# A hybrid decoder trunk on one core: a reworked router chain with the second expert's later loads held behind the first gather, and the last norm with ScalarE taking the moments of five tiles

## The reference

```
scores = softmax(x @ router_w + router_b)                      # 1024 tokens x 16 experts
grouped = scores.reshape(n_tok, 4, 4)
group_score = sum(top_k(grouped, 2)[0], -1)
sel = argmax(group_score)                                      # one group for each token
top_vals, top_idx = top_k(grouped[sel], 2)                     # two experts of that group
gates = top_vals / sum(top_vals)
moe = sum over the two experts of gate * ((silu(x @ w_gate[e]) * (x @ w_up[e])) @ w_down[e])
out = layer_norm(alpha * x + moe, ln2_g, ln2_b)                # mean and variance over 1024 columns
```

## Time and profile before

| | |
|---|---|
| runs | 1371.47, 1374.96, 1375.51 us |
| profiled execution | 1372.77 us, span 1370.7 us |
| granted clock, mean | 0.971 |
| PE busy | 1268.2 us (93%) |
| DVE busy | 511.4 us (37%) |
| ACT busy | 349.3 us (25%) |
| POOL busy | 108.1 us (8%) |
| moved by DMA | 170.17 MB, mean 124 GB/s |

### The profile page before, as it was taken

One profiled execution on the slowest core, in us unless ns is written; L12 is line 12 of the kernel. 1 busy time (PEld: TensorE's weight loads), 2 busy tenths in 40 slices (PEclk: granted clock), 3 DMA queues, 4 the chain that ended last, 5 costly groups with the idle time before them and its releaser, 6 DMA issues.

```text
span 1370.7 us, 23143 instructions
## 1 busy us (share of the span) xinstructions
PE 1268.2 (93%) x9642; PEld 628.1 (46%) x9642; DVE 511.4 (37%) x934; ACT 349.3 (25%) x482; POOL 108.1 (8%) x177
## 2 busy tenths in 40 slices
PE   7999999999999999999999964999999999999960
PEld 3444444444577777777445532333333333333320
DVE  3035310344178887886355355111111111110118
ACT  1044302234134433345221112111111111111114
POOL 1000000000111111010000001011101010101010
PEclk9999999999999999999999986999999999999985
DMA  5110010010000000001704008866789499397135
...
DMA packets 61012, 170.17 MB, mean 124 GB/s; under 512 B 3184, under 2 KB 3312, under 8 KB 60928
## 3 DMA queue, kind: packets, MB, share of 16 engines
...
...
## 4 chain that ended last, share of the span: by engine, by line
PE 86%; DVE 5%; ACT 4%; DMA 2%; issue 2%; SPq 0%; POOL 0%; POOLq 0%; DVEq 0%; ACTq 0%
PE PS L1762 32%; PE PS L204 19%; PE PS L1251 8%; PE PS L643 6%; PE PS L213 3%; PE PS L954 2%; PE PS L966 2%; PE PS L976 2%; PE PS L1755 2%; PE PS L347 1%; PE PS L1391 1%; PE PS L739 1%; DMA XS<-in_xT 1%; ACT XS L999 1%; PE PS L692 1%
## 5 line engine op out<-in xcount | busy, mean ns | idle before, releaser
L204 PE MATMUL PS<-XS 128*128 128x512 f32 x672 | 294.5, 598 | 7.3 <-DMA XS<-in_xT 6.9
L1762 PE MATMUL PS<-XS,YT 128*64 128x512 f32 x656 | 287.6, 596 | 0.9 <-DVE YT L1843 0.9
L1762 PE MATMUL PS<-SQ,YT 128*64 128x512 f32 x488 | 216.0, 596 | 0.0
L1762 PE MATMUL PS<-RK,YT 128*64 128x512 f32 x672 | 211.1, 593 | 0.0
L204 PEld LDWEIGHTS PS<-XS 128*128 128x128 f32 x672 | 127.2, 191 | 172.8 <-issue 164.0
L1762 PEld LDWEIGHTS PS<-XS,YT 128*64 128x64 f32 x656 | 89.0, 138 | 183.0 <-issue 181.9
L1850 DVE TENSOR_TENSOR YT<-YT,PS 128x256 f32<-128x256 f32 x42 | 15.8, 417 | 271.8 <-PE PS L1762 271.8
L1251 PE MATMUL PS<-SQ,YT 128*128 128x512 f32 x256 | 114.0, 594 | 0.0
L643 PE MATMUL PS<-XS 64*64 64x64 f32 x2880 | 101.2, 221 | 4.4 <-ACT XS L782 2.6
L1762 PEld LDWEIGHTS PS<-RK,YT 128*64 128x64 f32 x672 | 65.9, 137 | 74.8 <-issue 74.8
L643 PEld LDWEIGHTS PS<-XS 64*64 64x64 f32 x2880 | 90.2, 135 | 21.4 <-issue 13.1
...
## 6 DMA issues: line engine op xcount, KB each, us to landing
...
XS<-in_w_down SPq DMA_DIRECT2D x5, 2048.0 KB, 10.2
...
```

The source lines that it names most:

```text
L204: m = e.matmul(acc[:, half * HB:(half + 1) * HB], XS[:, 8 + n % 4, kt * P:(kt + 1) * P], XS[:, kt, half * HB:(half + 1) * HB], start=kt == ...
L1762: ins = e.matmul(acc[r, :], rows[:, r], third_cols(n, k, at, HB), start=start, stop=stop)
```

## The change

Three things change.

1. **The router.** The scores are no longer normalised (the gates are ratios, and the choice does not depend on the scale). The two largest of each group come from four maxima and minima of halves instead of a search, the chosen group's four scores are gathered into `cand` (4 columns for each tile instead of 16), and their ranks follow from all pairs at once (`earlier` breaks ties). `am` is bfloat16. TensorE adds up the counts over the tiles itself (8 small matmuls into 16 columns), and the places with their base (8 more), where VectorE had 8 additions. The path of the counts (`halves`, `key`, the pairs) goes ahead of that of the places (`pos_i`, `pos_h`, `pos`). GpSimd has five more small operations in `router_pool`.
2. **The loads.** Before n=1, the up third of the first pair's k=1, SyncE waits for the first gather (`wait(e, s_xg, 16)`). The gate third of k=1 is still issued at once.
3. **The last norm.** VectorE takes the moments of tiles 0 to 2 and then applies every tile in two passes, (x - mean) * gain and then * root + bias. ScalarE takes the moments of tiles 3 to 7 (a pass for the sum, a small product, a pass for the sum of squares), and all roots. Its pass that applied scale and shift is gone.

```diff
+            e.memset(onesb, 1.0)
+            e.memset(earlier, 1.0)
+            e.memset(key[:, 0:1], 0.0)
+            e.iota(rank_of, [[1, 2], [1, G_E]], base=1 - G_E, channel_multiplier=0, allow_small_or_imprecise_dtypes=True)
...
+            e.affine_select(out=earlier, in_=earlier, compare_op=ALU.is_gt, fill=0.0, base=0,
+                            pattern=[[-1, G_E], [1, G_E]], channel_multiplier=0)
+            e.affine_select(out=beforeb, in_=onesb, compare_op=ALU.is_gt, fill=0.0, base=0,
                             pattern=[[1, P]], channel_multiplier=-1).then_inc(s_rpool, 1)
...
-            step(RED(c8[0], te(pr), AX.X, ALU.add))
-            step(e.reciprocal(c8[1], c8[0]))
-            step(TTo(te(pr), te(pr), over(c8[1], E_N), ALU.mult))
-            step(RED(q1, pr.rearrange("p (q e) -> p q e", e=G_E), AX.X, ALU.max))
             quad = lambda x: x.rearrange("p (q e) -> p q e", e=G_E)
-            step(TTo(quad(k16), quad(pr), over(q1, G_E), ALU.is_equal))
-            step(TTo(quad(k16), quad(k16), under(rev4, NT * E_G), ALU.mult))
-            step(RED(q2, quad(k16), AX.X, ALU.max))
-            step(TTo(quad(k16), quad(k16), over(q2, G_E), ALU.is_equal))
-            step(e.scalar_tensor_tensor(pm, k16, -2.0, pr, ALU.mult, ALU.add))
-            step(RED(q2, quad(pm), AX.X, ALU.max))
+            duo = lambda x: x.rearrange("p (q h) -> p q h", h=2)
+            def go(ins):
+                ins.then_inc(s_q, 1)
+                n[0] += 1
+            go(TTo(duo(hi), quad(pr)[:, :, 0::2], quad(pr)[:, :, 1::2], ALU.max))
+            step(TTo(duo(lo), quad(pr)[:, :, 0::2], quad(pr)[:, :, 1::2], ALU.min))
+            go(TTo(over(q1, 1), duo(hi)[:, :, 0:1], duo(hi)[:, :, 1:2], ALU.max))
+            go(TTo(over(q2, 1), duo(hi)[:, :, 0:1], duo(hi)[:, :, 1:2], ALU.min))
+            step(TTo(over(q3, 1), duo(lo)[:, :, 0:1], duo(lo)[:, :, 1:2], ALU.max))
+            step(TTo(q2, q2, q3, ALU.max))
             step(TTo(q1, q1, q2, ALU.add))
...
+            square = lambda x: x.rearrange("p (i a b) -> p i a b", a=G_E, b=G_E)
+            turned = lambda x: x.rearrange("p (i a b) -> p i b a", a=G_E, b=G_E)
+            rows = lambda x: x.rearrange("p (i a o) -> p i a o", a=G_E, o=1).broadcast_to([P, NT, G_E, G_E])
+            cols = lambda x: x.rearrange("p (i o b) -> p i o b", o=1, b=G_E).broadcast_to([P, NT, G_E, G_E])
             step(TTo(quad(pm), quad(pr), over(g4, G_E), ALU.mult))
-            step(e.tensor_scalar_add(k4, g4, -1.0))
-            step(TTo(quad(pm), quad(pm), over(k4, G_E), ALU.add))
+            step(RED(quad(cand), turned(pm), AX.X, ALU.add))
+            step(TTo(square(k16), rows(cand), cols(cand), ALU.is_ge))
+            step(TTo(te(k16), te(k16), under(earlier, NT), ALU.mult))
+            step(TTo(square(pm), square(k16), turned(k16), ALU.subtract))
+            step(RED(quad(rank4), turned(pm), AX.X, ALU.add))
+            both4 = lambda x: x.rearrange("p (k i b) -> p k i b", k=2, b=G_E)
+            twice4 = lambda x: x.rearrange("p (o i b) -> p o i b", o=1, b=G_E).broadcast_to([P, 2, NT, G_E])
+            step(TTo(both4(oh4), twice4(rank4),
+                     rank_of.rearrange("p (k o b) -> p k o b", k=2, o=1).broadcast_to([P, 2, NT, G_E]), ALU.is_equal))
+            step(TTo(either, oh4[:, 0:NT * G_E], oh4[:, NT * G_E:], ALU.add))
+            wait(e, s_q, n[0])
+            TTo(square(am), rows(g4), cols(either), ALU.mult).then_inc(s_qd, 1)
             for k, oh in enumerate((oh1, oh2)):
-                step(RED(c8[k], te(pm), AX.X, ALU.max))
-                step(TTo(te(k16), te(pm), over(c8[k], E_N), ALU.is_equal))
-                step(TTo(te(k16), te(k16), under(rev16, NT), ALU.mult))
-                step(RED(c8[2], te(k16), AX.X, ALU.max))
-                step(TTo(te(oh), te(k16), over(c8[2], E_N), ALU.is_equal))
-                if k == 0:
-                    step(e.scalar_tensor_tensor(pm, oh, -4.0, pm, ALU.mult, ALU.add))
-            step(TTo(am, oh1, oh2, ALU.add))
-            wait(e, s_q, n[0])
-            e.memset(base[:, 0:E_N], 0.0).then_inc(s_qd, 1)
-            step(TTo(c8[2], c8[0], c8[1], ALU.add))
+                go(TTo(square(oh), rows(g4), cols(oh4[:, k * NT * G_E:(k + 1) * NT * G_E]), ALU.mult))
+            step(TTo(both4(top), both4(oh4), twice4(cand), ALU.mult))
+            two_tops = gate.rearrange("p k i -> p (k i)")
+            step(RED(two_tops, quad(top), AX.X, ALU.add))
+            step(TTo(c8[2], gate[:, 0, :], gate[:, 1, :], ALU.add))
             step(e.reciprocal(c8[2], c8[2]))
-            for k in range(2):
-                step(TTo(gate[:, k, :], c8[k], c8[2], ALU.mult))
+            step(TTo(gate, gate, under(c8[2], 2), ALU.mult))
             out_bias(e, NT - 1)
             e.wait_ge(s_qp, 1)
-            for i in range(NT):
-                step(TTo(base[:, (i + 1) * E_N:(i + 2) * E_N], base[:, i * E_N:(i + 1) * E_N],
-                         PS[2][:, i * E_N:(i + 1) * E_N], ALU.add))
-            count = base[:, NT * E_N:]
-            step(TTo(pos_i, PS[3][:, 0:NT * E_N], base[:, 0:NT * E_N], ALU.add))
-            step(e.tensor_single_scalar(pos_h, pos_i, 6, ALU.logical_shift_right))
-            step(e.scalar_tensor_tensor(pos, pos_h, float(C), pos_i, ALU.mult, ALU.add))
+            count = PS[2][:, 0:E_N]
             step(e.tensor_scalar_add(n_int, count, float(C - 1)))
             step(e.tensor_single_scalar(n_int, n_int, 6, ALU.logical_shift_right))
             step(e.tensor_scalar_max(halves, n_int, 1.0))
-            step(e.scalar_tensor_tensor(key, halves, float(E_N), rev16, ALU.mult, ALU.add))
-            step(e.memset(key[:, 0:1], 0.0))
+            step(e.scalar_tensor_tensor(key[:, 1:], halves[:, 1:], float(E_N), rev16[:, 1:], ALU.mult, ALU.add))
...
+            e.wait_ge(s_qp, 2)
+            step(e.tensor_copy(pos_i, PS[3][:, 0:NT * E_N]))
+            step(e.tensor_single_scalar(pos_h, pos_i, 6, ALU.logical_shift_right))
+            step(e.scalar_tensor_tensor(pos, pos_h, float(C), pos_i, ALU.mult, ALU.add))
...
             e.wait_ge(s_qd, 2)
-            e.matmul(PS[2][:, 0:NT * E_N], ones, am, start=True, stop=True)
-            e.matmul(PS[3][:, 0:NT * E_N], before, am, start=True, stop=True).then_inc(s_qp, 1)
+            for i in range(NT):
+                ins = e.matmul(PS[2][:, 0:E_N], onesb, am[:, i * E_N:(i + 1) * E_N], start=i == 0, stop=i == NT - 1)
+            ins.then_inc(s_qp, 1)
+            e.matmul(PS[3][:, 0:NT * E_N], beforeb, am, start=True, stop=False)
+            for i in range(1, NT):
+                ins = e.matmul(PS[3][:, i * E_N:NT * E_N], onesb, am[:, 0:(NT - i) * E_N], start=False, stop=i == NT - 1)
+            ins.then_inc(s_qp, 1)
...
+                if n == 1:
+                    wait(e, s_xg, 16)
...
+        BY_DVE = 3
+        spare = SQ[:, 4, :]
+        def final_moments_dve(e, i):
+            x, st, m = FIN[i], stats[:, i % 2, :], mv[:, i, :]
             wait(e, s_gt[i], 16)
             for half in range(2):
                 ins = e.bn_stats(st[:, 6 * half:6 * half + 6], x[:, half * HB:(half + 1) * HB])
             ins.then_inc(s_f1, 1)
...
+            wait(e, s_f1, 2 * i + 1)
             e.bn_aggr(m[:, 0:2], st).then_inc(s_f1, 1)
...
+        def final_moments_act(e, i):
+            x, m, n = FIN[i], mv[:, i, :], i - BY_DVE
+            wait(e, s_gt[i], 16)
+            wait(e, s_f2, 3 * n)
+            e.activation(spare, x, ACT.Identity, accum_out=m[:, 3:4]).then_inc(s_f2, 1)
+            wait(e, s_f2, 3 * n + 1)
+            e.mul(m[:, 0:1], m[:, 3:4], 1.0 / D).then_inc(s_f2, 1)
+            wait(e, s_f2, 3 * n + 2)
+            e.activation(spare, x, ACT.Square, scale=-1.0, bias=m[:, 0:1], accum_out=m[:, 1:2]).then_inc(s_f2, 1)
+        def final_root(e, i):
+            m = mv[:, i, :]
+            if i < BY_DVE:
+                wait(e, s_f1, 2 * (i + 1))
+            else:
+                wait(e, s_f2, 3 * (i - BY_DVE + 1))
+            e.activation(m[:, 2:3], m[:, 1:2], ACT.Ln, scale=1.0 if i < BY_DVE else 1.0 / D, bias=consts[:, 3:4])\
+             .then_inc(s_n2a, 1)
+            wait(e, s_n2a, 2 * i + 1)
+            e.activation(m[:, 2:3], m[:, 2:3], ACT.Exp, scale=-0.5).then_inc(s_n2a, 1)
+        def final_apply(e, i):
+            x, m = FIN[i], mv[:, i, :]
+            wait(e, s_n2a, 2 * (i + 1))
+            e.scalar_tensor_tensor(x, x, m[:, 0:1], LN2[0], ALU.subtract, ALU.mult).then_inc(s_f3, 1)
             wait(e, s_f3, i + 1)
...
+            e.scalar_tensor_tensor(x, x, m[:, 2:3], LN2[1], ALU.mult, ALU.add).then_inc(s_f4, 1)
         def final_dve(e):
             e.wait_ge(s_l2, 32)
...
+            for i in range(BY_DVE):
+                final_moments_dve(e, i)
+            for i in range(NT):
+                final_apply(e, i)
+        def final_act(e):
+            for i in range(BY_DVE):
+                final_root(e, i)
+            for i in range(BY_DVE, NT):
+                final_moments_act(e, i)
```

(1 more changed line is left out.)

55 lines of the change are left out of this document (10 added, 45 removed).

## The result

The changed kernel takes 1361.53 us (median of 4 runs, 1359.74 to 1363.21); the kernel before took 1375.17 us beside it (median of 4 runs). The ratio of the two is 0.9907 with a 95% interval of 0.9885 to 0.9929, so it is **12.8 us faster (9.8 to 15.8)**; between the medians lie 13.6. In a second comparison it took 1361.31 us (4 runs) and the ratio was 0.9904 (0.9888 to 0.9921). The forecast was 1362.5 us in a range of 1357 to 1368, faster with a chance of 0.92.

A forecast was written before the change was run, and what follows sets the result against it. TensorE's matmul rounds bound the kernel and stay; only the stretches before and after them can change. Front 5.0 plus last norm 6.4 gives 11.4 us: 1361.4 from the profiled time, 1363.6 from the median, so 1362.5, range 1357 to 1368.

The forecast's parts named there:

- the front: All before the first round's down matmuls: 5.0 us gained, from 4.6 router, 0.8 gather, 1.7 clock, less 2.1 stall.
- The router: VectorE's steps before the first gather: fewer and narrower operations bring the table 4.6 us earlier (4.1 to 5.0).
- they end before the table does: SyncE's stores to `sums`, following `out_bias` 2.9 us earlier, were to end before VectorE's table and so delay nothing.
- The gather: Load of the first rows before the rounds: 8.2 us from its issue instead of 8.97, so 0.8 gained.
- Now only the gate third is there: Reason given for the shorter first gather: up and down thirds no longer queue behind the gate third beside it.
- holding back does not do what it says: Rival on the first gather: it still takes 8.97 us, crowded by the gate third alone; 0.8 back, 1363.3 us; chance 0.15.
- The new stall: Before the first up matmuls: TensorE waits 2.1 us for the up third, issued only after the gather lands.
- The clock: TensorE's first gate matmuls: a gap of 1.2 us instead of 2 keeps the 2.4 GHz level, 1.7 us gained.
- The last norm: After the last round: VectorE's two passes take 2.52 us a tile, 6.4 us gained if ScalarE keeps up.
- ScalarE: Its chain in the last norm: 3.2 us a tile, at most 3.6, taken as hidden with 1 us to spare.
- The half-speed summing pass: Rival: ScalarE bounds the last norm, summing passes taking 2.4 us instead of 1.15; kernel about 1374 us; chance 0.04.
- VectorE at half rate: Rival: VectorE's two last-norm passes take 5.1 us a tile, ending 14 us later than before; kernel 1382 us; chance 0.01.

The follow-up runs named there:

- the trace with all thirds held: The changed kernel with the wait for the first gather put before all three thirds, the gate third's too: 1365.33 us, ratio 0.9946.
- the unheld runs of the new router: Kernels with the changed router whose up third does not wait for the gather, with the old or a new last norm: medians from 1359.02 to 1367.61 us.
- last norm alone: The kernel before with only the changed last norm put in: 1367.77 us, ratio 0.9957.
- the one with two tiles for VectorE: The changed kernel without the wait, VectorE taking two tiles' moments and ScalarE six, ScalarE's product kept: 1361.25 us, ratio 0.9917.
- The hold alone: The kernel before with only the up third's wait for the first gather added: 1374.82 us, ratio 1.0011.
- the one with 24 matmuls: The kernel before with 24 instead of 16 matmuls in `keep_clock`, ahead of the transposes: 1372.8 us, ratio 0.9989.
- the second pair: The kernel before and the changed kernel, each unaltered and profiled a second time: 1373.32 us and 1361.31 us.

## Why the prediction was right or wrong

The time, the sign and the range were right, and the sum for the front (5.0) came out at 5.04 in the two profiled executions. The sum hides that two of its terms, the gather and the clock, were put down to the wrong thing: that it came out so near is in part luck.

- **The router** (4.6 forecast) gave 4.88 in that pair; over all traces it is 28.37 to 28.43 us against 23.39 to 23.50. `out_bias` came 6.93 us after the router's start instead of 7.3: operations without a wait between them started 0.10 to 0.14 us apart, not 0.2 as counted. The matmuls and GpSimd's operations cost nothing, as said: from L1568 (now L1580) to the gather's issue are 10.38 us before and 10.39 after. What was said of SyncE's stores ("they end before the table does") holds for their issue and not for their landing. Before, the last one was issued at 833.9 and landed after 5.5 us at most, ahead of the gather's issue; in the trace with all thirds held, which has the changed kernel's times here, it landed 2 us behind it. The gate third stands behind these stores in SyncE's queue, and that may be why it took 11.0 to 11.6 us in the unheld runs of the new router where the forecast had 10.2, and why TensorE waited 1.50 and 1.15 us for it in two of them. But it took 11.2 once with the old router too (last norm alone), and no run here parts the two.
- **The gather** (0.8 forecast, 0.73 in the pair): right size, wrong mechanism. The step that failed is "Now only the gate third is there", taken as the reason. Without the hold the changed kernel's transposes came as early in one trace (8.28), and 0.67 us later in the one with two tiles for VectorE (8.96), whose code is the same up to that place. With the old router they came, unheld, after 9.02, 9.03 and 9.98, and held after 8.55, so there the step may hold. The greater part of the gather's time comes with the gate third beside it: 4.36 us without, 8.25 with. That also breaks the lower bound of the forecast, "hardly under 5 us", drawn from a load of the same 0.5 MB at 4.2. Why the new router's unheld gathers are shorter than the old one's (8.28 to 8.96 against 9.02 to 9.98) is open: no run here parts them.
- **The rival "holding back does not do what it says"** (0.15) was right for the changed kernel in its mechanism, to within a quarter of a microsecond, and wrong in its price (8.97; it took 8.25). With the new router, what stands behind the gate third in SyncE's queue took next to nothing from the gather in GpSimd's queue: 8.28 to 8.96 with it, 8.29 and 8.45 without. The Trainium skill (DMA: Bandwidth & Descriptors, Queues, rings and completion order) has each DMA engine go round robin between queues. These traces agree with it, and so does the run without the gate third beside the gather (4.36 against 8.25); the one held trace of the old router (8.50 against 8.97 to 9.94) leans the other way.
- **The new stall** (2.1 forecast) is there: 2.17 and 1.91 and 1.70 us in three traces, with the up third landing 10.50 us after its issue instead of 10.2. The argument that it comes whatever the gather takes holds. It was priced well and its meaning missed: a wait that costs 2 us and buys a quarter is a loss. The hold alone made the kernel before slower by 1.5 us (0.3 to 2.7).
- **The clock** (1.7 forecast, 1.56 in the pair) was booked as a gain of every execution, and it is one of a single trace. The step that failed is to take the one profiled execution's fall at 850.7 for what the kernel before does: its second execution, the one with the new last norm and the one with 24 matmuls kept the clock on the same code or nearly so. What the forecast said of the gap fits all fourteen traces as far as they go (a gap of 2.00 ahead of the transposes was followed by the fall, gaps of 0.52 to 1.54 were not), but the gap depends on when the 2.4 GHz level comes back within `keep_clock`, and that differs from execution to execution. How often before loses the clock there, and whether the change makes it rarer, no run settles. Where the clock holds in both, as in the second pair, the front is worth 28.40 + 26.74 less 23.50 + 28.05, or 3.6 us, not 5.0.
- **The last norm** (6.4 forecast) gave 7.18: mis-sized by 0.8. The pitch of 2.52 us is exact, 8 tiles took 1355.90 - 1335.73 = 20.17. The term that was off is tile 2's arrival: forecast 3.5 us after the first statistics, it was there by 1334.34, 2.84 us after. In after's second trace it came late (VectorE waited 0.21 us) and the stage took 24.7 us. Half a microsecond was given back in the other direction, since the first tile came 9.97 us after the last scatter instead of 9.47.
- **ScalarE** was forecast at 3.2 us a tile and took 3.11, with 1.39 us to spare at the last tile (1 forecast). The half-speed summing pass of that rival does not exist; the sum costs one more instruction of 0.18 us for each pass. **VectorE at half rate**: 1.28 us for the form with two float32 sources, beside 1.22 for the plain tensor_tensor. The Trainium skill (Vector Engine (DVE) Microarchitecture Reference, Points that are easy to get wrong) has this form at half throughput; this trace does not agree.

The parts measured one by one give 5.5 + 5.9 - 1.5 = 9.9 us, the whole 12.8 (9.8 to 15.8). The traces give 3.6 for the front and 6.9 to 7.2 for the last norm, so 10.5 to 10.8 where the clock holds, and 1.6 more against an execution of before that loses it. That lies within the interval; whether the 2 us up to 12.8 are more than that clock loss and chance, no run settles.
